# A decoder step with 32 experts: a ring of 18 weight slots, rotation on VectorE, norms from sums of squares, a router on the raw tile

## What is computed

```
logits = h @ w_router + b_router                      # h: 288 x 1024, 32 experts
top_val, top_e = top_k(logits, 4); gates = softmax(top_val)
gate, up = split(x_e @ w_gu[e] + b_gu[e])             # 1024 -> 2 x 1024
act = (min(gate, 7) * sigmoid(1.702 * gate)) * (clip(up, -7, 7) + 1)
out += gates[e] * (act @ w_down[e] + b_down[e])       # 1024 -> 1024
```

## Time and profile before

| | us |
|---|---|
| median of 3 runs (1482.79 to 1485.16) | 1484.63 |
| the profiled execution | 1483.09 |
| its span, first to last instruction | 1481.2 |
| TensorE busy | 1249.4 (84%) |
| VectorE busy | 426.0 (29%) |
| ScalarE busy | 312.0 (21%) |
| GpSimd busy | 245.5 (17%) |
| DMA queue of the loads, share of 16 engines | 80.9% |

### The profile page before, as it was taken

How to read it: one execution, slowest core, us unless ns; L and a number is a source line. 1 busy time by engine, 2 the same in 40 slices (tenths; PEclk the granted TensorE clock), 3 DMA queues, 4 the chain that set the end, 5 groups by cost and what they waited for, 6 DMA issues and landing times.

```text
span 1481.2 us, 33684 instructions
## 1 busy us (share of the span) xinstructions
PE 1249.4 (84%) x13199; PEld 685.5 (46%) x13200; DVE 426.0 (29%) x940; ACT 312.0 (21%) x629; POOL 245.5 (17%) x541
## 2 busy tenths in 40 slices
PE   8998889998794997888989887797887978879873
PEld 6786666776462452343435343342432523424231
DVE  2125444124346431222313222121221312222116
ACT  1234433013215221111112121111111211112012
POOL 2000000000011321222222121222211212213122
PEclk9999899999996999899999999998998989989887
DMA  9326268433875499979797999999999999999994
GB/s 295 116 87 231 86 215 301 131 125 139 269 292 235 188 416 418 418 298 419 310 417 311 417 419 418 419 416 417 418 419 416 417 419 418 417 417 418 418 418 189
DMA packets 117498, 481.63 MB, mean 325 GB/s; under 512 B 8042, under 2 KB 40978, under 8 KB 84466
## 3 DMA queue, kind: packets, MB, share of 16 engines
q1 hardware_dynamic: 115682, 475.43, 80.9%
q0 software_dynamic: 1728, 5.53, 1.1%
q10 hardware_dynamic: 48, 0.13, 0.0%
HBM read 475.42 MB, written 5.64 MB: 325 GB/s over the span
## 4 chain that ended last, share of the span: by engine, by line
PE 44%; DMA 24%; SPq 17%; DVE 8%; issue 4%; ACT 2%; DVEq 0%; POOL 0%; ACTq 0%; POOLq 0%
PE bank L1061 13%; DMA area<-in_w_down 12%; PE bank L534 12%; DMA ring<-in_w_down 11%; SPq L1150 10%; SPq L1148 6%; PE bank L1084 5%; PE bank L543 4%; DVE area L2286 2%; PE bank L524 2%; ACT area L1401 1%; PE bank L862 1%; PE bank L706 1%; DMA ring<-in_cache_mem_v 1%; DVE area L2301 1%
## 5 line engine op out<-in xcount | busy, mean ns | idle before, releaser
L1061 PE MATMUL bank<-ring,area 128*32 128x512 f32 x2432 | 329.9, 672 | 78.7 <-DMA ring<-in_w_gu 78.7
L2297 DVE TENSOR_SCALAR area<-bank 128x256 f32<-128x256 f32 x51 | 21.7, 425 | 737.5 <-PE bank L1061 737.5
L1061 PEld LDWEIGHTS bank<-ring,area 128*32 128x32 f32 x2432 | 75.2, 115 | 305.6 <-DMA ring<-in_w_gu 190.1
L1401 ACT ACTIVATE area<-bank 128x256 f32<-128x256 f32 (+5 forms) x299 | 122.9, 446 | 422.0 <-PE bank L1084 206.4
L534 PE MATMUL bank<-ring 128*128 128x288 f32 x640 | 159.6, 410 | 4.1 <-DMA ring<-in_w_in 1.6
L1084 PE MATMUL bank<-ring,area 128*32 128x256 f32 x2240 | 132.8, 381 | 20.9 <-DMA ring<-in_w_down 12.6
L2286 DVE TENSOR_TENSOR area<-area,bank 128x512 f32<-128x512 f32 (+1 forms) x255 | 143.4, 627 | 2.0 <-PE bank L1000 2.0
L534 PEld LDWEIGHTS bank<-ring 128*128 128x128 f32 x640 | 122.5, 192 | 39.0 <-issue 2.5
L1061 PE MATMUL bank<-area 128*32 128x512 f32 x832 | 108.0, 643 | 26.0 <-DMA area<-in_w_gu 26.0
L1355 POOL TENSOR_SCALAR area<-consts,area 128x128 f32<-128x128 f32 x156 | 122.5, 795 | 11.2 <-POOL area L1351 11.2
L1758 ACT ACTIVATE area<-area 128x256 f32<-128x256 f32 x51 | 21.3, 417 | 487.5 <-DVE area L2297 487.5
(11 more groups left out here) (226 smaller groups left out, 1138.5 us busy)
## 6 DMA issues: line engine op xcount, KB each, us to landing
ring<-in_w_gu SPq DMA_DIRECT2D x192, 1024.0 KB, 19.2
ring<-in_w_down SPq DMA_DIRECT2D x96, 1024.0 KB, 20.0
area<-in_w_gu SPq DMA_DIRECT2D x64, 1024.0 KB, 15.0
area<-in_w_down SPq DMA_DIRECT2D x32, 1024.0 KB, 26.0
ring<-in_w_in SPq DMA_DIRECT2D x12, 1024.0 KB, 9.5
ring<-in_w_mkv SPq DMA_DIRECT2D x8, 1024.0 KB, 10.6
ring<-in_cache_k SPq DMA_DIRECT2D x16, 512.0 KB, 5.8
ring<-in_cache_v SPq DMA_DIRECT2D x16, 512.0 KB, 6.4
```

The costliest lines, as they stand in the source:

```text
L1061: last = pe.matmul(bank[1][CAP * j:CAP * j + CAP, :], xgT[:, k, :], quarter(w, j), start=False, stop=(k == KB - 1))
L1401: return act.activation(out, in_, ACT.Copy, scale=scale)
```

## The change

- **Ring.** `ALL` = 18 (two more slots in `area`, where the routing's scratch lies until the order of the experts is known). Experts 0 and 1 come first, the other 30 are ordered, in turns of 3. SyncE waits for the order before the 17th load; TensorE waits for it before the third expert.
- **Rotation.** VectorE forms the sine product directly from PSUM, reading the rows 32 away, in four operations of 32 rows; no copy, no rotation matrix. Queries lie in `qT` without zeros; `score` multiplies each head on its 64 rows, and a PSUM bank holds one head's scores (384 columns).
- **Norms.** Inverse roots as `exp(-0.5 * ln(x))` on ScalarE, in place of square root and reciprocal. Layer norm: sums of y and of y squared together, variance from their difference. In the second, GpSimd centres half the tile.
- **Router.** The router weights are scaled by the norm's gain and centred over the features ahead of time; TensorE multiplies them with the raw tile beside the sums, and the logits are that, times the inverse root, plus a bias. Sample tokens are replicated on four groups of rows in the same matmuls, so that VectorE works on all rows at once.
- **Token split.** Ranks come ahead of the token turns; the turns go by feature half, ScalarE makes the first parts early and the scaled copies late.
- **Expert stage.** GpSimd picks a block's bias rows after the gather rather than after the turned gates.
- **Tail.** Inverse root as in the norms.

The core of the diff:

```diff
-ALL = 16
-GROUP = 4
+EARLY_ALL = 16
+ALL = 18
+FIRST = 2
+GROUP = 3
...
-            at = AREA - (ALL - i) * SLOT
+            at = AREA - (EARLY_ALL - i if i < EARLY_ALL else ALL + 4 - i) * SLOT
...
-            sp.wait_ge(blocks_ready, 1)
-            for i in range(ALL, GROUP * CHUNKS_E):
...
             sp.wait_ge(order_ready, 1)
-            with sp.Fori(1, NE // GROUP) as group:
+            for i in range(EARLY_ALL, ALL):
+                chunk(1, i)
+            before = blocks_before(0)
+            for i in range(ALL, FIRST * CHUNKS_E):
+                slot_free(before, i - ALL)
+                chunk(1, i)
+            with sp.Fori(0, (NE - FIRST) // GROUP) as turn:
...
             def score(p):
...
+                halves_of = [open_fill(("s", p, hh)) for hh in range(2)]
+                for q0, n_keys, at in ((0, P, 0), (P, 256, P)):
+                    for hh, (ps, full) in enumerate(halves_of):
+                        rows = slice(HD * hh, HD * hh + HD)
+                        last = pe.matmul(ps[:, at:at + n_keys], qT[rows, p, q0:q0 + P], kT[rows, p, 0:n_keys], start=True, stop=True)
...
+            def rotate(kind, m, out):
+                ps = await_fill(dve, (kind, m))
...
+                step(dve.tensor_tensor(rope_t[:, 0, :], ps[:, 0:T], C("cos"), ALU.mult))
+                for a in range(0, P, 32):
+                    b = a ^ 32
+                    step(dve.tensor_tensor(rope_t[a:a + 32, 1, :], ps[b:b + 32, 0:T], C("sin")[b:b + 32, :], ALU.mult))
...
+            def inverse_root(out, in_, bias=0.0):
+                step(act.activation(out, in_, ACT.Ln, bias=bias))
+                settle()
+                return act.activation(out, out, ACT.Exp, scale=-0.5)
...
+            def norm_parts(n, kind):
+                parts = [open_fill((name, n)) for name in ("mean part", "sq part")]
+                if n == 1:
+                    parts.append(open_fill(("lg part",)))
...
-            load_table(ACT.Sqrt)
+            load_table(ACT.Ln)
...
-                act.activation(small[0:r, 24 + c:25 + c], small[0:r, 17 + 2 * c:18 + 2 * c], ACT.Sqrt, bias=eps_col(LN_EPS, r)).then_inc(fin_root, 1)
+                step(act.activation(root, var, ACT.Ln, bias=eps_col(LN_EPS, r)))
+                settle()
+                act.activation(root, root, ACT.Exp, scale=-0.5).then_inc(fin_root, 1)
```

More of the change, by code:

```diff
@@ L126, in const_table @@
     put("diag4", np.where(r[:, None] // CAP == r[None, :] // CAP, slots, -1000))
-    put("eye3", np.tile(np.eye(32), (3, 1)))
-    rest = NE - GROUP
+    put("eye4", np.tile(np.eye(32), (4, 1)))
+    put("caps", CAP * np.arange(1, MORE + 1)[None, :].repeat(P, 0))
+    rest = NE - FIRST
     odd = list(range(1, rest, 2))
@@ L824, in _ @@
                 used(("w", "mq", i))
+                if i == 0:
+                    pe.wait_ge(router_go, 1)
+                    ps, full = open_fill(("router mean",))
+                    pe.matmul(ps[:, 0:NE], C("one"), router_sum, start=True, stop=True).then_inc(full, 1)
             for m in range(KB):
@@ L1164, in _ @@
             sp.wait_ge(bias_split, 1)
-            for i in range(RING, ALL):
+            for i in range(RING, EARLY_ALL):
                 chunk(1, i)
@@ new lines, in _, with layer_norm @@
+                inverse_root((rstd, lnv)[g], ps[:, 0:T], eps_col(RMS_EPS)).then_inc(read_sem(("rms", g)), 1)
+            def layer_norm(n, kind, out, gamma, beta, mid, between):
+                for m in range(KB):
+                    await_read(act, (kind, m))
+                    act.activation(sqT[:, m, :], yT[:, m, :], ACT.Square).then_inc(sq_ready, 1)
+                part_in(("mean part", n))
+                mid()
+                ps = await_fill(act, ("mean", n))
+                if n == 1:
+                    copy(mean_s, ps[:, 0:T])
+                act.activation(mean_sq, ps[:, 0:T], ACT.Square).then_inc(mean_ready, 1)
+                act.wait_ge(var_ready, n + 1)
+                inverse_root(rstd, rstd).then_inc(rstd_ready, 1)
+                for m in range(KB):
+                    act.wait_ge(norm_mul, 4 * n + m // 2 + 1)
+                    act.activation(out[:, m, :], yT[:, m, :], ACT.Identity, bias=vec[:, beta + m:beta + m + 1],
+                                   scale=vec[:, gamma + m:gamma + m + 1]).then_inc(norm_done, 1)
+                    if m == 3:
+                        between()
@@ L2191, in _ @@
             settle()
-            for j in range(1, REPS):
-                step(copy(rankm[NS * j:NS * j + NS, 2, :], rankm[0:NS, 2, :]))
-            step(copy(nblk_at[0:1, 0:GROUP], nxf[0:1, 0:GROUP]))
+            step(copy(nblk_at[0:1, 0:FIRST], nxf[0:1, 0:FIRST]))
             step(dve.tensor_reduce(total_f, nxf[0:1, :], AX, ALU.add))
```

625 lines of the change are left out of this document (295 added, 330 removed).

## The result

The changed kernel takes 1449.18 us (median of 4 runs, 1448.48 to 1450.18), the kernel before, on the same chip, 1483.85 us (1482.79 to 1485.16). The ratio is 0.9766, with a 95% interval of 0.975 to 0.9783. The profiled execution of the changed kernel took 1448.48 us with a span of 1446.7 us, so the span shrank by 34.5 us. TensorE's mean granted clock was 0.93.

What follows compares the result with a forecast made beforehand. The expert weight stream at 418 GB/s was taken as the bound, its start and standstills deciding. Terms summed to -35.7 us, span 1481.2 to 1445.5, plus 1.9 and 1.5 us: 1449 us, range 1443 to 1454.

Steps and rivals of the forecast that it cites:

- projections, with ScalarE's wait and two score pairs: Before prompt attention: rotation on VectorE -3.9 us, ScalarE's query copies gone -0.6, two score pairs side by side -1.3.
- prompt attention, three rounds: Closed chain of three rounds: shorter scores start ScalarE's absolute value 0.6 us earlier each, -1.7 us (-0.3 to -2.5).
- RMS norm and layer norm 1: The two early norms: TensorE is busy 46.95 of 48.0 us there, so 0 us, -1 to +1.
- router stage: Last projection's end to first expert matmul: logits 10.7 us earlier, then token split copies late; -9.8 us (-7 to -12).
- ring: Expert weight loads, 18 slots for 16: three stalls 5.0 us shorter each, two loads in the idle gap; -20.1 us.
- tail: Last norm: logarithm and exponential replace root and reciprocal, with added table loads; +1.7 us, bounds 0 and +2.8.
- the two gap loads: Expert stream: two more loads go out in the idle gap before 500 us instead of in the stream, 5.0 us.
- Rival 3: Ring: issue order, not depth, holds the queue, so only the idle gap's 5 us come; 1464 us, chance 0.04.
- rival 1: Early savings eaten: order late, heads not overlapping, router gains only 7; around 1456 us, 1459 at worst, chance 0.2.
- rival 4: Expert stage: TensorE becomes the bound if its clock stays at 1.2 GHz; 1513 us, chance 0.02.
- Rival 2: Router, tail, RMS norm: logarithm and exponential find one table, saving loads; 1445 us, chance 0.08.
- A score pair: TensorE's scores of two heads run side by side on half the rows each: 0.65 us for 1.31.

Runs made afterwards that it cites:

- the three edits together: Changed kernel with the memory value projection ahead of the turned probabilities, last norm's root by Sqrt and reciprocal, and three scaled token copies on VectorE: 1438.68 us.
- The filled run: Changed kernel with 10 more 128x256 matmuls after the scores of the third and the fifth head pair, into an unread bank: 1446.1 us, ratio 0.9732.

## Why the prediction was right, and where it was not

1449 us was forecast, with a range of 1443 to 1454, and 1449.18 measured. The sum was -35.7 us and the span shrank by 34.5. That the two numbers agree to 0.2 us is luck: the steps below miss by +0.1, +3.4, -1.1, -1.0, -0.85, +1.0 and -0.3 us, which cancel to 1.2, and the median lay 0.7 us above the profiled execution where 1.5 had been added. Counted from stage border to stage border, in the order of time:

| step | forecast | measured | read from |
|---|---|---|---|
| projections, with ScalarE's wait and two score pairs | -5.8 | -5.7 | first turned probabilities, from 120.85 to 115.15 |
| prompt attention, three rounds | -1.7 | +1.7 | 197.92 to 193.88, less the above |
| RMS norm and layer norm 1 | 0 | -1.1 | 302.10 to 296.98, less the above |
| memory attention up to the end of y2 | none | -1.0 | 438.28 to 432.19, less the above |
| router stage | -9.8 | -10.65 | first expert matmul, 482.04 to 465.30, less the above |
| ring | -20.1 | -19.1 | last landing, 1457.13 to 1421.25, less the above |
| tail | +1.7 | +1.4 | last landing to the end, 24.07 to 25.46 |

Of these steps the ring, the prompt attention and the tail were tested by runs; the shares of the projections and of the router stage as a whole are read from the two traces alone.

**The ring was right in mechanism and size.** Three stalls shrank, by 6.5, 4.8 and 4.9 us, where 3 x 5.0 stood in the sum; undone alone the ring costs 19.6 us at the last landing, held back alone the two gap loads cost 4.7. Rival 3, that the order and not the depth holds the queue, falls with both runs. Two new gaps, 3.98 us at 562.30 and 3.64 at 599.72, are together 2.6 us longer than two loads and give back most of what the stalls gained beyond the sum. No condition of rival 1 came true (the order was in time, the heads overlap, the router stage gave more than 7), and rival 4 neither: the stream still runs at 418 GB/s to its last load, and the tail follows that.

**The router stage was right, and 0.9 us better than forecast.** Counted from the end of the projections, the logits came after 10.5 us (442.70; the sum had 11.7), the last of ScalarE's copies of the token split that VectorE waits for ended after 27.6 us (459.79), the last that the gather waits for after 29.0 us (461.20; the sum had 28.7 for the last copy), and the first expert matmul stood after 33.1 us (34.0). So the logits' lead was lost at the copies, and what is left was won behind the gather. That ScalarE's copies set the gather held: TensorE waited 7.55 us for them, and the stretch became 1.7 us shorter when three of the scaled copies went to VectorE (the three edits together). Rival 2 is refuted by the loads at 436.75 and 438.87. The Trainium skill, page "ScalarE: Activation LUTs", section "Table sets: the hidden batching unit", gives one load for a logarithm and an exponential; the trace doesn't agree for this program, which has one at each change, 1.28 us each.

**The prompt attention is the step that failed**: a gain of 1.7 us was forecast and 1.7 were lost, a miss of 3.4 us. It said that the shorter scores bring ScalarE's absolute value 0.6 us closer to their start, from 2.19 us to 1.6. It is 2.26 and 1.95 us in the two rounds shown and 1.94 in the third. The sum let ScalarE's copies start 0.65 us after the scores' start; they start 1.31 and 1.00 us after it. Before, the pair's banks filled one after the other, so that ScalarE copied the first (0.38 us) while TensorE still filled the second. Now each head has a bank and both are full at the end, so that both copies (0.87 us) stand behind the scores. Most of TensorE's gain went into ScalarE's lost overlap. Whether banks filled by query tile would bring both was not tried. Then the step's neighbour: shorter scores lengthen the idle stretch behind them, to 4.58 and 4.34 us, and what follows it runs longer at the lower clock. The filled run shows that this, and not the chain, made the rounds longer. The forecast priced the scores alone and did not ask what TensorE does with the time that it wins ahead of a wait.

How much was lost depends on where the clock falls, and that varies between executions of the same order. The three rounds took 66.7 us in the kernel before and 68.4 in the changed one; in the other runs that leave the rounds as they are, or exchange only the heads' order, they took 66.7, 68.3, 67.0, 66.8 and 68.5 us. So the gain of 1.7 us came in none of six, and the loss lies between 0 and 1.8.

**A score pair** was forecast at 0.65 us and costs 0.83: two visible pairs take 1.66 from 92.15 to 93.81, against 2.62. The records of the two halves start 0.006 us apart, so they do overlap. About 0.1 us goes with the first record (0.21 us to the next, where the other records of 128 columns are followed after 0.11) and 0.24 us between the last record and the projection behind it; why is not shown. The term was 0.3 us too large; the projections made it up elsewhere.

**Layer norm 1** was forecast at nothing, with bounds of 1 us for both early norms, and gave 1.6: TensorE works without a gap from 280.01 to 296.98. Its 0.9 us of waits are gone, and its sums of the norm take 0.4 us less. The bound was read from TensorE's idle time and left out that its own work could shrink. The RMS norm, in the same row of the table, lost 0.5 us, so that the two together end just past the bound; TensorE's wait for the RMS norm's products grew from 0.93 to 1.30 us.

**The memory attention** itself was not changed. Its stretch was 1.0 us shorter because behind its wait for a load (4.38 us, before 4.49) the clock stood at the lower level from 394.2 to 397.6 us, before from 398.0 to 404.8: the matmuls there took 3.35 and 1.97 us instead of 3.64 and 2.69. By the varying clock of the rounds above, this too may be chance.

**The tail** went by its steps: both chunks behind the first have two loads each, and the second load of the last chunk ends at 1440.09, 0.24 us before VectorE's offset. ScalarE and VectorE in the tail:

```profile
1430.05 1.28 ACT L1805 ACT_TABLE_LOAD   x1
...
1438.81 1.28 ACT L1807 ACT_TABLE_LOAD   x1
...
1430.54 5.18 DVE L2371 COPY area<-area 32x256 f32<-32x256 f32 x4
...
1440.33 0.15 DVE L2356 SCALAR_TENSOR_TENSOR small<-small 32x1 f32<-32x1 f32 x1 [3.01 <-ACT small L1807]
```

## What to carry to other kernels

Where a stream of loads is the bound, price a change by the stream's start and by each place where its queue stands still, and check each place by undoing that part alone. When a step on TensorE ahead of a wait becomes shorter, ask what is idle longer, and look for independent work that can be issued ahead of the wait; here that move was worth 9.4 us, where the shorter step itself won nothing. Before work is added to fill a gap, count instructions and not records, and measure the gap and the work in the same trace.

## What the runs showed of the hardware

- TensorE's granted clock falls to its lower level (1.2 GHz) behind short idle stretches, and which stretch it is varies from run to run: behind 3.02 us of idling the same projection took 3.69 us in one run and 6.75 in another. With the stretches filled, all windows from 110 to 200 us stood at a granted clock of 1.00, the 2.4 GHz level. The Trainium skill, page "TensorE: Matmul & The Clock Gate", section "HAM oscillation — how this bites in real kernels", warns of idle gaps between bursts of matmuls, behind which the clock has fallen, and advises a loop order by which TensorE stays at the full clock; these runs agree.
- VectorE's operations from SBUF to SBUF can stand still beside GpSimd's: 1.05 us beside a subtraction on GpSimd and 0.31 without it; four copies of 32x256 in 5.17 us beside two operations of 2.34 us, and 1.73 us on ScalarE beside the first of them. In that last run VectorE's offset, 0.16 us elsewhere, took 1.70 us and ended at 1421.39, 0.01 us after GpSimd's operation (1419.04 to 1421.38). The Trainium skill, page "SBUF — State Buffer", section "SBUF: two separate sides", describes a port pair that the two engines take from each other for whole instructions; both places agree. In the tail it was worth 3.0 us (24.38 to 21.40).
- Matmuls on the two halves of the rows overlap whether they are issued in turns or one half after the other: a pair took 0.93 us on TensorE's row in both orders, where the full rows took 1.31.
